# Split weights in slots 4160 instead of 4096 bytes apart, y and hid at another remainder of 512 bytes

## The reference, cut to what matters

```
h = rms_norm(x, norm1_w)
p = h @ w_in                                    # 2048 x 6152
y = concat(mLSTM(p), diff_attention(p))         # 256 x 2048
x = x + y @ w_out                               # 2048 x 2048
h = rms_norm(x, norm2_w)
x = x + (silu(h @ w_gate) * (h @ w_up)) @ w_down    # 2048 x 5632 twice, 5632 x 2048
```

## The kernel before, in words

| operand | before | after |
|---|---|---|
| act_hi, act_lo (stationary) | 128 | 128 |
| y_hi, y_lo, hid_hi, hid_lo (stationary) | 256 | 128 |
| w_hi, slots 0 to 3 (moving) | 128, 128, 128, 128 | 128, 192, 256, 320 |
| w_lo, slots 0 to 3 (moving) | 128, 128, 128, 128 | 384, 448, 0, 64 |

## Time and profile before

### The profile page before, as it was taken

The page is one execution under the profiler, slowest core; times in us unless marked ns, Lnnn a source line. Parts: engine busy times, 40 slices in busy tenths (PEclk is TensorE's granted clock), DMA queues, the critical chain, the costliest instruction groups (busy, mean ns, idle before and its releaser), DMA issues.

```text
span 1149.3 us, 14440 instructions
## 1 busy us (share of the span) xinstructions
PE 1130.5 (98%) x5064; PEld 930.3 (81%) x5064; DVE 600.8 (52%) x685; ACT 537.8 (47%) x665; POOL 4.5 (0%) x20
## 2 busy tenths in 40 slices
PE   6999999899999999999999999999999999999998
PEld 5888887788888888888888888888888888888886
DVE  5576466564665655455454554554554544454443
ACT  7565476554554454444444444434444433333331
POOL 1000000000000000000000000000000000000000
PEclk9999999999999999999999999999999999999999
DMA  9555444554455556555555555555555555555554
GB/s 350 185 177 186 149 147 142 177 178 162 159 171 187 179 172 211 185 185 198 182 183 201 181 200 185 183 198 183 185 199 182 185 186 197 184 185 194 187 184 128
DMA packets 59651, 212.45 MB, mean 185 GB/s; under 512 B 6736, under 2 KB 6736, under 8 KB 59616
## 3 DMA queue, kind: packets, MB, share of 16 engines
q1 hardware_dynamic: 59408, 211.84, 54.0%
q10 hardware_dynamic: 144, 0.05, 0.0%
q0 software_dynamic: 64, 0.07, 0.0%
HBM read 209.83 MB, written 2.10 MB: 184 GB/s over the span
## 4 chain that ended last, share of the span: by engine, by line
PE 96%; DVE 2%; ACT 1%; issue 0%; DMA 0%; ACTq 0%
PE acc L378 27%; PE acc L381 27%; PE acc L380 27%; PE aux L381 4%; PE aux L378 4%; PE aux L380 4%; PE aux L392 2%; DVE w_lo L898 1%; DVE conv L1066 0%; DMA xt<-in_x_turned 0%; PE aux L442 0%; ACT w_hi L645 0%; DVE res L1208 0%; PE aux L494 0%; ACT conv L779 0%
## 5 line engine op out<-in xcount | busy, mean ns | idle before, releaser
L898 DVE TENSOR_TENSOR w_lo<-w_raw,w_hi 128x1024 fp32r<-128x1024 f32 x392 | 478.5, 1225 | 459.0 <-ACT w_hi L652 338.9
L378 PE MATMUL acc<-w_lo,act_hi 128*128 128x512 f32 x1088 | 429.5, 395 | 13.4 <-DVE w_lo L898 13.4
L652 ACT ACTIVATE w_hi<-w_raw 128x1024 fp32r<-128x1024 f32 x256 | 271.3, 1061 | 364.9 <-PE acc L381 227.2
L381 PE MATMUL acc<-w_hi,act_hi 128*128 128x512 f32 x1088 | 425.0, 391 | 0.0
L380 PE MATMUL acc<-w_hi,act_lo 128*128 128x512 f32 x1088 | 424.7, 390 | 0.0
L378 PEld LDWEIGHTS acc<-w_lo,act_hi 128*128 128x128 f32 x1088 | 205.0, 188 | 57.3 <-issue 10.8
L381 PEld LDWEIGHTS acc<-w_hi,act_hi 128*128 128x128 f32 x1088 | 205.1, 188 | 43.3
L380 PEld LDWEIGHTS acc<-w_hi,act_lo 128*128 128x128 f32 x1088 | 205.2, 189 | 41.5
L645 ACT ACTIVATE w_hi<-w_raw 128x1024 fp32r<-128x1024 f32 x136 | 141.9, 1057 | 81.2 <-PE acc L381 72.1
L378 PE MATMUL acc<-w_lo,hid_hi 128*128 128x512 f32 x176 | 69.5, 395 | 0.0
L378 PE MATMUL aux<-w_lo,hid_hi 128*128 128x512 f32 x176 | 69.5, 395 | 0.0
(11 more groups left out here) (191 smaller groups left out, 534.1 us busy)
## 6 DMA issues: line engine op xcount, KB each, us to landing
w_raw<-in_weights SPq DMA_DIRECT2D x392, 512.0 KB, 3.3
res<-in_x SPq DMA_DIRECT2D x4, 512.0 KB, 9.7
out<-res SPq DMA_DIRECT2D x8, 256.0 KB, 3.8
xt<-in_x_turned SPq DMA_DIRECT2D x3, 512.0 KB, 8.1
xt<-in_x_turned SPq DMA_DIRECT2D x2, 256.0 KB, 4.8
w_if<-in_gate_w POOLq DMA_DIRECT2D x1, 64.0 KB, 5.9
par<-in_params ACTq DMA_DIRECT2D x1, 47.0 KB, 4.3
bias_if<-in_gate_bias POOLq DMA_DIRECT2D x1, 0.0 KB, 5.5
```

The lines of the kernel that those rows point to most:

```text
L378: pe.matmul(bank[:], hi[:, k, tok], w_lo[:, slot, cols], start=first and kk == 0, stop=False)
L381: mm = pe.matmul(bank[:], hi[:, k, tok], w_hi[:, slot, cols], start=False, stop=last and kk == len(kts) - 1)
L652: act.activation(w_hi[:, c % SPLIT, :], w_raw[:, c % RAW, :], ACT.Copy).then_inc(hi_done, 1)
L898: dve.tensor_tensor(w_lo[:, slot, :], w_raw[:, slot, :], w_hi[:, slot, :].bitcast(F32), ALU.subtract).then_inc(lo_done, 1)
```

## The change

The rows of w_hi and w_lo get 16 floats more, which nobody reads or writes, so that the four slots are 4160 bytes apart; the copy and the subtraction are told to take the first 1024 floats. `line_pad` grows from 24 to 120 floats: with the 512 bytes that w_hi and w_lo have grown by, y and hid move from 256 to 128 past a multiple of 512. No instruction is added, removed or moved to another place in its engine's order.

```diff
-        w_hi = sb("w_hi", [SPLIT, CH], F32R)
-        w_lo = sb("w_lo", [SPLIT, CH], F32R)
+        w_hi = sb("w_hi", [SPLIT, CH + 16], F32R)
+        w_lo = sb("w_lo", [SPLIT, CH + 16], F32R)
...
-        sb("line_pad", [24])
+        sb("line_pad", [24 + 96])
...
-                act.activation(w_hi[:, slot, :], w_raw[:, slot, :], ACT.Copy).then_inc(hi_done, 1)
+                act.activation(w_hi[:, slot, 0:CH], w_raw[:, slot, :], ACT.Copy).then_inc(hi_done, 1)
...
-                act.activation(w_hi[:, c % SPLIT, :], w_raw[:, c % RAW, :], ACT.Copy).then_inc(hi_done, 1)
+                act.activation(w_hi[:, c % SPLIT, 0:CH], w_raw[:, c % RAW, :], ACT.Copy).then_inc(hi_done, 1)
...
-                dve.tensor_tensor(w_lo[:, slot, :], w_raw[:, slot, :], w_hi[:, slot, :].bitcast(F32),
+                dve.tensor_tensor(w_lo[:, slot, 0:CH], w_raw[:, slot, :], w_hi[:, slot, 0:CH].bitcast(F32),
                                   ALU.subtract).then_inc(lo_done, 1)
```

## The result

The changed kernel takes 1161.3 us (1161.21 to 1161.38), the kernel before 1150.8: ratio 1.0093, 95% interval 1.0081 to 1.0106. It is 10.5 us slower, where 8.2 us faster was forecast. (The size of 0.9% is small, but the interval doesn't touch 1, and each of the two kernels agrees with itself within 1 us.)

What follows compares the result with a forecast made beforehand. PE was taken as the bound, through the time from one matmul's start to the next. From the profiled 1151.05 us, 8.2 for y and hid and 0 for the stagger gave 1142.85, forecast as 1142.6 us; range 1137 to 1165.

Steps and rivals of the forecast that it cites:

- y and hid from 256 to 128: y and down stages: 1440 matmuls fall from 0.2324 to act's 0.2267 us, saving 5.7 ns each, 8.2 us.
- I take zero: All 4704 weight matmuls: slots 4160 bytes apart cost nothing, set between a 3.3 us gain and an 18.6 us loss.
- the upper bound of the loss: Shifted slots: 5.7 ns on each of 3264 act matmuls, 18.6 us, with none of the 8.2 us gained.
- the gate matmuls L402 and L403: 256-column matmuls, stationary starts at eight remainders of 512: 0.1194 us each, none standing out; taken as nearest row for the stagger.
- Rival 1: Weight matmuls: distance between the two operands counts, so act loses its even pace; 1164.8 to 1169.4 or 1152.7 to 1156.0; chance 0.39.
- Its signs: Rival 1 would show in ff intervals of 0.229 to 0.233 us, different from slot to slot or uneven within a chunk.
- the forecast's own: Whole kernel: range 1140.5 to 1146 us around the forecast of about 1142.6; chance 0.38.
- The covers: Slower copies or subtractions would hide in VectorE's 338.9 us and ScalarE's 227.2 us of waits, about 1.5 us per chunk.
- The rule against it: TensorE's independent read ports mean no placement matters: sum zero, time 1150.8 us; given a small chance.

Runs made afterwards that it cites:

- the distances tried above: Against the kernel with only y and hid moved to 128, y and hid shifted by own pads to distances 16 to 240; 1151.35, 1151.5, 1154.13 and 1150.41 us.

## Why the prediction was wrong

- **y and hid from 256 to 128: right.** 1440 x 5.7 ns = 8.2 us; alone it gave 1150.75 - 1142.99 = 7.8 us, with the pace as forecast. But the reason was wrong. 128 isn't a better place than 256; it was the place of the weights, and only with the weights still there does it help. The sum came out for this part because both readings give it, the right one and the wrong one.
- **The step that failed is "I take zero", the price of the stagger.** It costs 1161.3 - 1143.0 = 18.3 us. That it looks like the upper bound of the loss (18.6) is chance: that bound was for act alone, with the 8.2 us of y and hid lost besides, 26.8 against the forecast. Nor was 5.7 ns the worst there is: act has 232.9 - 226.7 = 6.2 ns in slots 2 and 3, and the distances tried above go up to 234.3. The measured sum is another one: all 4704 matmuls pay 231.1 - 226.7 = 4.4 ns, which is 20.7 us against an even pace without a break; the runs after transposes, which are uneven in any kernel, take some of it back, above all in the input projection with its many interruptions (4.0 us for 1152 x 4.4 ns = 5.1). y and hid lose the 5.7 ns that the other part gave them except for 1.3.
- **Why I took zero:** the gate matmuls L402 and L403 show no bad distance among eight. The row was read rightly and carried too far. They are 256 columns wide, and at this width distance 128 costs nothing over distance 0 (118.7 or 120.0 against 120.0 ns). Besides, the eight are only four distances modulo 256: 32, 96, 160 and 224. None of those that the change makes (0, 64, 128, 192) is among them, and at 512 columns these four lie at 233.3, 233.3, 234.3 and 233.3 ns, nearly alike and all bad. That sweep would have looked flat even at full width, without a row at distance 0 to compare it with. I had called it a weak row and yet let it set the term. The nearer row was in the text: the earlier trace rows are a distance of 128 at full width, and the stagger puts one slot in four exactly there.
- **Rival 1 was the mechanism**, at 0.39 a little above the forecast's 0.38, with its sizes off. It took the distance without the modulus, so that w_lo and w_hi of one slot would differ, where modulo 256 they have the same distance; it had y and hid keep 0.2324 (they took the common 0.2311), and the time at 1164.8 to 1169.4, or 1152.7 to 1156.0 if half of the slots stayed even. One slot in four did, with a restart to pay, and the time lies between. Its signs came as written: distances of 0.229 to 0.233 us, other ones from slot to slot. The wide range, 1137 to 1165, holds the measured time only because this rival was let into it; the forecast's own, 1140.5 to 1146, misses it by 15 us.
- **The covers held.** Copies and subtractions took what they took, and no new wait of PE appeared. (Two readings of the earlier trace rows were a point off, without weight: 100.02 and 84.80 of 220 us are 45% and 39%.)
- **The rule against it.** By "PE and ACT never wait on anyone" ("SBUF — State Buffer", section "Who interferes with whom", of the Trainium skill), as the prediction applied it, placement wouldn't matter. The runs disagree, by 7.8 us for a pad of 384 bytes in front of y and hid. But that part of the page speaks of one engine against another, and what is seen here is PE against itself: the chunks of ff keep their length to a nanosecond whatever ScalarE, VectorE and the loads do beside them. The rule of the skill's "TensorE: Matmul & The Clock Gate", section "Wait — 56ns, not 53.3ns?", N / 2.4 GHz + 2.5 ns, gives 215.8 and 109.2 ns; the best even paces measured with fp32r are 226.7 and 120.0.

What stays open is what in TensorE makes the distance count: that it counts is shown, why is not. It isn't the amount that a load reads (half the load doesn't halve the excess), not the load under the stream alone, and it depends on the length of the stream. The even paces are multiples of one step: 226.67 = 34 x 6.667 ns, 233.33 = 35 x 6.667, 120.0 = 18 x 6.667, where 6.667 ns is 16 columns, 64 bytes, at 2.4 GHz. The uneven paces fit it too, by whole turns of their pattern: 7 x 232.38 = 244 steps at distance 128, 3 x 228.89 = 103 at 64, 7 x 234.29 = 246 at 160, 5 x 118.66 = 89 with 256 columns. That suggests a raster on which the matmuls fall, but no run separates it from other explanations, and none shows what makes one turn longer than another or which of two paces a stretch takes.

The fastest kernels of the study are the three with all distances 0 modulo 256, 1142.4 to 1143.0 us; of these the pad of `line_pad` alone is the simplest.

## What to carry to other kernels

For fp32r matmuls of 512 columns, each with its own stationary operand of 128 columns, put the moving and the stationary operand at starts that are equal modulo 256 bytes, in every slot of a ring: a slot pitch that is a multiple of 256 keeps it, a pitch of 64 or 128 more breaks it, for 18 and 14 us here. Don't carry it to 256 columns, where distance 128 was no worse. When one and the same matmul has two paces in one trace, compare the places of both its operands, and read the start-to-start distances, not the durations. And a row of another width isn't evidence for a price that may depend on the width, nor is a flat sweep evidence of no price when it doesn't hold the case that it is compared with.

## What the hardware showed beyond that

- The pace is a state. After transposes even the best distance runs uneven for some ten matmuls, after a slot of another distance for three to five; then it is 226.67 ns (2720 ns for every one of the 153 ff chunks of the kernel before that hold no transpose). At distances 16 and 240, at 128 with 256 columns, and in ff of the kernel with w_lo alone shifted, one and the same code has two steady paces, which change at interruptions alone.
- It doesn't follow the other engines: the 12 distances of a chunk repeat while ScalarE, VectorE and the loads come and go.
- The odd multiples of 32 bytes are the worst (233.3 and 234.3 ns), with 192 as bad (233.3), and a shift by 16 bytes is not symmetric: 226.7 or 228.3 on one side, 226.7 or 233.3 on the other.
- With 64 stationary columns the same stream is slower than with 128 (230.0 for 226.7 ns at distance 0).
- At the 1.2 GHz level nothing comes on top: the eleven distances of 427 ns at the start of the changed kernel are 512 columns at 1.2 GHz, 426.7.
